# Low parts of the normalized tiles all on VectorE; norm sums, statistics and vector products rearranged through PSUM

## The chip, the cores and the metric

The kernel runs on one core of a Trainium2 chip. The metric is the device time of one execution in microseconds (us); lower is better. The program is one launch that works through two stacked networks of two layers each.

## The reference

```
# block 1, two layers (x: 512 tokens x 1024 features)
h = x @ w_in                         # split into three mixers' inputs
mix = concat(stick_breaking(h_sb), latent_attention(h_mla), rwkv7(h_rwkv)) @ w_o
x = layer_norm(ALPHA * x + mix, ln1_g, ln1_b)            # norms 0 and 2
u_act, u_gate = split(x @ ffn_w_up)
hid = gelu(causal_conv3(u_act)) * u_gate
x = layer_norm(ALPHA * x + hid @ ffn_w_down, ln2_g, ln2_b)  # norms 1 and 3
# block 2, two layers
h = modulate(rms_norm(x)); x = x + gate * mixer(h)       # norms 4 and 6; RG-LRU, then pooling
h = modulate(rms_norm(x)); x = x + gate * relu(h @ w1)**2 @ w2   # norms 5 and 7
out = rms_norm(x)                                        # norm 8
layer_norm(x) = (x - mean) * rsqrt(var + eps) * g + b    # over the 1024 features
```

## The kernel before, in words

**Layout.** Features lie on the partitions: `x` is 8 tiles of 128 features x 512 tokens. A weight matrix comes from HBM as a stream of chunks; a chunk holds 8 blocks of 128x128, by which it makes one tile of 128 output features. Two slots (`raw[:, 0]` and `raw[:, 1]`) alternate.

**Split products.** Each product is made of three fast ones (`split_product`, L668 to L670): both operands are split into a high part (`wh`, `xh`, `hidh`, rounded to fp32r) and a low part (`wl`, `xl`, `hidl`, the rest), and high x high, high x low and low x high are added up in PSUM. ScalarE makes `wh` of a chunk from `raw` (L1538, a whole chunk; L1552 and L1564, half chunks), then VectorE makes `wl` (L2361; L2374 and L2387, half chunks). `lo_done` tells TensorE and the DMA queue that a chunk is split.

**Order.** Each engine runs its own program, written out by hand, and engines meet at counting semaphores. Within a dense stretch TensorE works on two PSUM banks in turn, `dbank[0]` for even and `dbank[1]` for odd chunks (`dense`); before it writes a bank it waits on `bank_free[j]`, which whoever reads the bank last counts up.

**The deferred norms (0, 1, 2 and 5).** The first two chunks behind a norm are not made from the normalized input. `ahead_pair` multiplies `x * g` (not centred, not scaled) into `AHEAD` = `aux[0]`, `aux[1]` while the norm's sums are still being made; the missing terms follow from two vectors, `-g` and `b`, that are multiplied by the same weights. These vector products are two small matmuls behind each weight block (L793, L798: the weight block is loaded, 4 and 2 columns of `vcol` are streamed) and give columns in `COLS` = `aux[2]`. `ahead_out` adds the columns' parts (L2466) and computes `(x_product + mean * col) * rstd` into `ahead_t` (L2458, L2459). After the first half of a chunk TensorE counts `pe_half`, so ScalarE and VectorE can split the first half of the chunk after next (`early_half`); the rest follows after `pe_chunk` (`rest`).
`spread` (L772) is a matmul with a matrix of ones that adds 128 partitions' sums and spreads them: sum of `x` to `aux[5]`, sum of squares to `aux[4]`. `turned_pair` then multiplies the next two chunks into `TURNED` = `aux[3]`, `aux[4]`, in order of the tiles: for each normalized tile both chunks' blocks. After that TensorE makes chunks 5 and 6 of the stage (counted from 1) in `dbank[0]` and `dbank[1]`, each in one go, and before the change waits in front of them only for readers of before the norm (`pl.use(s + j, 1) - 2`).
`turned_tiles` on VectorE makes the tiles: `centre` (L2422, x - mean), `scale` (L2489, x g rstd), the low part `xl` (L2499); ScalarE makes `xh` with `b` (L1628).

**GpSimd's part.** It adds up `norm_sum` (L3333) and, for norm 1 and others, `norm_sq` (L3341). In norms 0 and 2 the squares' sum is VectorE's (L2967). GpSimd also makes three of the eight low parts, tiles 1, 3 and 5 (`POOL_LOW`; L3324), for which ScalarE first adds `b` to `x` itself (L1631). For the other five tiles ScalarE does that afterwards (`shift_tile`, L1641).

**Who reads the turned banks.** In the feed-forward of layers 1 and 2, VectorE reads `TURNED[1]` as the gate of hidden tile 1 (L3047). In layer 2's projections ScalarE reads it into `sbq` (L1729), behind the two `cq` (L1694), `ckv` (L1697), the five shifts (L1641), a wait for GpSimd's copy of the layer's vectors (L3352, which itself waits for the shifts) and three squares (L1711 to L1713). In norm 5's stage ScalarE reads it in a Relu (L2281).

Of the kernel before, what the change touches and what calls it, by code (L numbers as in the profile page):

```python
# [18 lines left out]
F32 = mybir.dt.float32  # L19
# [100 lines left out]
def columns(vecs):  # L120
    at, out = 0, {}
    for name, n in vecs:
# [10 lines left out]
          ("eye2", 64), ("tri", 64), ("tri_incl", 64), ("upper_half", 1),  # L133
# [4 lines left out]
def constants():  # L138
# [12 lines left out]
    put("ones", np.ones((P, P)))  # L151
    r, t = i % HD, np.arange(HD)[None, :]
# [29 lines left out]
POOL_LOW = (1, 3, 5)  # L182
# [5 lines left out]
SUMS = (8, 8, 8, 8, 7, 8, 7, 0, 7)  # L188
SQ_SUMS = (7, 8, 7, 8)
# [80 lines left out]
def build(nc, x_in, stream, mod_stream, vecs1, vecs2, consts, bands, c_rows, out):  # L270
    ctx = ExitStack()
    with ctx:
# [50 lines left out]
        ahead_t = at("ahead_t", [P, 2, S], krv_at + 18432)  # L323
        wag_at = top[0]
# [150 lines left out]
        tile_used, ahead_ready = sem("tile_used"), sem("ahead_ready")  # L475
        mean_ready, mean_pe, centred_x = sem("mean_ready"), sem("mean_pe"), sem("centred_x")
# [27 lines left out]
        lb_masked, n_masked, lk_masked = sem("lb_masked"), sem("n_masked"), sem("lk_masked")  # L504
        eye_ready, pb_zero, inv_turned = sem("eye_ready"), sem("pb_zero"), sem("inv_turned")
# [24 lines left out]
        z_pe, z_out, pool_pe, sq_pe = sem("z_pe"), sem("z_out"), sem("pool_pe"), sem("sq_pe")  # L530
# [32 lines left out]
        AHEAD, TURNED, COLS = (aux[0], aux[1]), (aux[3], aux[4]), aux[2]  # L563
# [98 lines left out]
        def _(pe):  # L662
# [101 lines left out]
            def spread(k, square):  # L764

                if k in (0, 2) and square:
                    pe.wait_ge(sq_added, sq_sums_before(k) + 7)
# [8 lines left out]
            def ahead_pair(pl, s, n, k):  # L776
# [3 lines left out]
                mine = slice(0, 4) if k < 4 else slice(1, 4, 2)  # L780
                ours = slice(0, 2) if k < 4 else mine
                n_hi = 4 if k < 4 else 2
                pe.wait_ge(vec_ready, vecs_split(k))
                for half in range(2):
                    for j in range(2):
                        if half == 0:
                            pe.wait_ge(lo_done, pl.chunk(s + j) + 1)
                        for t in range(4 * half, 4 * half + 4):
                            if j == 0:
                                pe.wait_ge(xl_ready, low0 + t + 1)  # L790
                            split_product(AHEAD[j][:], ((s + j) % 2, t * P), slice(0, P),
                                          (h[:, t, :], l[:, t, :]), t == 0, t == KT - 1)
                            m = pe.matmul(COLS[:, 8 * j:8 * j + n_hi], wh[:, (s + j) % 2, t, :],  # L793
                                          vcol[:, t, mine], start=t == 0 and j == 0, stop=False,
                                          skip_group_check=True)
                            if j == 1 and k in IN_PLACE:
                                m.then_inc(tile_used, 1)
                            m = pe.matmul(COLS[:, 8 * j:8 * j + 2], wl[:, (s + j) % 2, t, :],  # L798
                                          vcol[:, t, ours], start=False, stop=t == KT - 1,
                                          skip_group_check=True)  # L800
                        m.then_inc(pe_half if half == 0 else pe_chunk, 1)
                        if half == 0 and j == 0 and k < 4:
                            spread(k, False)
                    if half == 0:
                        spread(k, True)

            def turned_pair(pl, s, n, tile):

                q = halves(n)
                for t in range(KT):  # L810
                    tile(t)
                    for j in range(2):
                        if t == 0:
                            pe.wait_ge(lo_half, 2 * q + j + 1)
                        if t == 4:
                            pe.wait_ge(lo_done, pl.chunk(s + j) + 1)
# [15 lines left out]
            def deferred(pl, s, n, k, count, tile):  # L832

                ahead_pair(pl, s, n, k)
                turned_pair(pl, s + 2, n, tile)
# [325 lines left out]
            def inverses(L, pl):  # L1161
# [36 lines left out]
                pe.wait_ge(pb_zero, L + 1)  # L1198
# [34 lines left out]
            def scan_chunks(L, b):  # L1233
# [6 lines left out]
                pe.wait_ge(lb_masked, k + 1)  # L1240
# [36 lines left out]
                pe.wait_ge(lk_masked, k + 1)  # L1277
# [47 lines left out]
            for L in range(DEPTH):  # L1325
# [5 lines left out]
                elif 1 in DEFERRED:  # L1331
                    behind = 2
                    ahead_pair(pl, C_MLA, L * 2, 1)
                    turned_pair(pl, C_MLA + 2, L * 2, shared_low(lows_before(1, True), 3))
# [152 lines left out]
            def pool_sums(m):  # L1487
# [3 lines left out]
                    .then_inc(sums_pe if m == KT - 1 else sq_pe, 1)  # L1491
# [37 lines left out]
        def _(act):  # L1529
# [37 lines left out]
            def square(k, m):  # L1567
# [3 lines left out]
                elif k in (0, 2):  # L1571
                    act.wait_ge(sq_added, sq_sums_before(k) + max(1, m - 2))
# [15 lines left out]
            def mean_stats(k):  # L1588

                act.wait_ge(mean_pe, k + 1)  # L1590
                act.activation(mean_t[:], aux[5][:], ACT.Copy, scale=1.0 / D)\
                    .then_inc(mean_ready, 1)
                act.activation(var_t[:], aux[5][:], ACT.Square, scale=1.0 / D)\
                    .then_inc(mean_ready, 1)

            def root_stats(k):
# [4 lines left out]
                act.activation(rstd_t[:], var_t[:], ACT.Exp, scale=-0.5).then_inc(rstd_ready, 1)  # L1601
# [13 lines left out]
            def between(pl, s, q, m):  # L1615

                if m in (0, 2):
                    rest(pl, s + m // 2)
# [3 lines left out]
            def turned_tiles(k, b, pl, s, q):  # L1622

                for m in range(KT):
# [8 lines left out]
                    between(pl, s, q, m)  # L1633
# [47 lines left out]
            def projections(L, pl):  # L1681
                behind = 2 if L and 1 in DEFERRED else 0
                if behind:
                    q = halves(L * 2)
                    early_half(pl, C_MLA, q, 0)
                    mean_stats(1)
                    early_half(pl, C_MLA, q, 1)
# [4 lines left out]
                    for j in range(2):  # L1692
                        act.wait_ge(ahead_ready, 2 * deferred_before(1) + j + 1)
                        act.activation(cq[:, j, :], ahead_t[:, j, :], ACT.Identity,  # L1694
                                       bias=small[:, 12, 4 * j + 1:4 * j + 2])\
# [240 lines left out]
            def scan_chunks(L):  # L1936
# [7 lines left out]
                for b in range(BLOCKS):  # L1944
                    act.wait_ge(p_pe, L * 4 + b + 1)
                    act.wait_ge(pb_zero, L + 1)
# [67 lines left out]
            for L in range(DEPTH):  # L2014
# [19 lines left out]
                if ahead:  # L2034
                    up = C_FFN[0][0]
                    early_half(pl, up, q, 0)
                    mean_stats(k)
                    early_half(pl, up, q, 1)
# [7 lines left out]
                for g, tiles in enumerate(GROUPS1):  # L2046
                    up, down = C_FFN[g]
                    for i in range(tiles):
# [11 lines left out]
                        if early_chunks and i == 0:  # L2060
                            act.wait_ge(ahead_ready, 2 * deferred_before(k) + 1)
                            act.activation(cv[:], ahead_t[:, 0, :], ACT.Identity,
                                           scale=vec("conv2", 0), bias=small[:, 12, 2:3])
# [20 lines left out]
                        if g == 0 and ahead and i >= 3:  # L2084
# [1495 lines left out]
```

## Time and profile before

| | us |
|---|---|
| median of 3 runs | 2384.37 (2382.88 to 2385.79) |
| the profiled execution's own time | 2383.53 |
| its span, first to last instruction | 2381.7 |
| TensorE busy | 2309.4 (97%) |
| VectorE busy | 1450.3 (61%) |
| ScalarE busy | 1028.9 (43%) |
| GpSimd busy | 276.2 (12%) |
| mean granted TensorE clock | 0.989 of full |

"Busy" counts the time in which an engine has an instruction in work; matmuls overlap, so a busy TensorE can still run at half its clock. The time outside the span is 1.8 us.

### The profile page before, as it was taken

What the parts mean: (1) busy time and instruction counts of PE and PEld (TensorE: products, weight loads), DVE (VectorE), ACT (ScalarE), POOL (GpSimd) and SP (SyncE); (2) the same over time, 40 slices, a digit from 0 to 9 for tenths busy, and PEclk for the clock granted to TensorE, in tenths of its full rate; (3) what the DMA queues carried; (4) which work ended last, traced back from release to release, by engine and by line L of the source; (5) the groups of instructions that cost most, each with busy time, mean ns of one, the idle gap of its engine ahead of it and who ended that gap; (6) DMA issues with size and microseconds to landing.
All of it is one profiled execution on the core that took longest, in us unless ns stands there. A gap on an engine that the chain in (4) does not pass through costs nothing.

```text
span 2381.7 us, 35746 instructions
## 1 busy us (share of the span) xinstructions
PE 2309.4 (97%) x13360; PEld 1856.7 (78%) x13360; DVE 1450.3 (61%) x1970; ACT 1028.9 (43%) x1603; POOL 276.2 (12%) x199
## 2 busy tenths in 40 slices
PE   8999999999999999999999998999999999999998
PEld 6777767888887777767888876778888888888887
DVE  4668678666577678688666556577444356443443
ACT  5667245333345667245333334665233243332332
POOL 0042221000042141220000040201000010000001
PEclk9999999999999999999999997999999999999999
DMA  4210014555432210014555431222322221223222
GB/s 162 80 62 28 29 45 159 194 194 193 162 106 82 87 54 28 29 45 168 197 191 193 159 109 36 80 94 94 106 96 94 94 96 62 89 97 97 97 97 88
DMA packets 68797, 248.33 MB, mean 104 GB/s; under 512 B 7632, under 2 KB 8144, under 8 KB 68688
## 3 DMA queue, kind: packets, MB, share of 16 engines
q1 hardware_dynamic: 68688, 246.85, 31.1%
q8 instruction: 72, 1.18, 0.2%
q14 instruction: 37, 0.30, 0.0%
HBM read 244.72 MB, written 2.10 MB: 104 GB/s over the span
## 4 chain that ended last, share of the span: by engine, by line
PE 48%; DVE 4%; ACT 2%; issue 1%; DVEq 0%; ACTq 0%
PE dense L668 15%; PE dense L669 14%; PE dense L670 14%; PE aux L853 1%; PE aux L668 1%; ACT wh L1538 1%; PE aux L669 1%; PE aux L670 1%; DVE wl L2361 1%; DVE xc L3116 0%; DVE xc L3083 0%; DVE xc L3082 0%; DVE xc L3081 0%; PE aux L1483 0%; DVE hidl L2396 0%
## 5 line engine op out<-in xcount | busy, mean ns | idle before, releaser
L1538 ACT ACTIVATE wh<-raw 128x1024 fp32r<-128x1024 f32 x338 | 358.0, 1059 | 866.9 <-PE dense L670 858.4
L668 PE MATMUL dense<-xh,wh 128*128 128x512 f32 x1712 | 685.1, 400 | 16.4 <-DVE wl L2361 11.5
L2361 DVE TENSOR_TENSOR wl<-raw,wh 128x1024 fp32r<-128x1024 f32 x338 | 427.1, 1264 | 410.7 <-ACT wh L1538 408.8
L670 PE MATMUL dense<-xh,wl 128*128 128x512 f32 x1712 | 668.0, 390 | 0.0
L669 PE MATMUL dense<-xl,wh 128*128 128x512 f32 x1712 | 667.5, 390 | 0.0
L668 PEld LDWEIGHTS dense<-xh,wh 128*128 128x128 f32 x1712 | 322.1, 188 | 104.1 <-issue 25.9
L669 PEld LDWEIGHTS dense<-xl,wh 128*128 128x128 f32 x1712 | 322.4, 188 | 69.4 <-issue 5.8
L670 PEld LDWEIGHTS dense<-xh,wl 128*128 128x128 f32 x1712 | 321.8, 188 | 68.0
L668 PE MATMUL dense<-hidh,wh 128*128 128x512 f32 x928 | 362.9, 391 | 4.9 <-DVE hidl L2396 2.1
L669 PE MATMUL dense<-hidl,wh 128*128 128x512 f32 x928 | 361.2, 389 | 0.0
L670 PE MATMUL dense<-hidh,wl 128*128 128x512 f32 x928 | 361.2, 389 | 0.0
L668 PEld LDWEIGHTS dense<-hidh,wh 128*128 128x128 f32 x928 | 174.1, 188 | 46.5 <-DVE hidl L2396 7.3
L670 PEld LDWEIGHTS dense<-hidh,wl 128*128 128x128 f32 x928 | 174.2, 188 | 36.4
L669 PEld LDWEIGHTS dense<-hidl,wh 128*128 128x128 f32 x928 | 174.2, 188 | 35.8
L3227 DVE SCALAR_TENSOR_TENSOR x<-dense,mod,x 128x512 f32 (+1 forms) x64 | 48.0, 751 | 179.7 <-PE dense L670 179.7
L3341 POOL TENSOR_TENSOR norm_sq<-norm_sq,sq 128x512 f32<-128x512 f32 x38 | 69.1, 1818 | 721.5 <-ACT sq L1577 721.5
L3005 DVE CUSTOM_DVE_ANT_0 mraw<-mraw,cond 128x1024 f32<-128x1024 f32 x96 | 117.0, 1218 | 0.0
L3333 POOL TENSOR_TENSOR norm_sum<-norm_sum,x 128x512 f32<-128x512 f32 x32 | 55.1, 1723 | 520.6 <-DVE x L2923 492.0
L2012 ACT ACTIVATE hidh<-hf 128x512 f32 (+1 forms) x108 | 68.1, 631 | 99.1 <-DVE hf L3203 92.7
L2396 DVE TENSOR_TENSOR hidl<-hf,hidh 128x512 f32 (+1 forms) x108 | 74.4, 689 | 59.8 <-ACT hidh L2012 59.8
L1577 ACT ACTIVATE sq<-x 128x512 f32<-128x512 f32 x64 | 39.9, 624 | 48.3 <-DVE x L2977 20.3
L668 PE MATMUL aux<-xh,wh 128*128 128x512 f32 x96 | 42.5, 442 | 5.5 <-POOL xl L3324 5.5
(445 smaller groups left out, 2745.0 us busy)
## 6 DMA issues: line engine op xcount, KB each, us to landing
raw<-stream SPq DMA_DIRECT2D x362, 512.0 KB, 3.4
mraw<-mod_stream SPq DMA_DIRECT2D x96, 512.0 KB, 4.3
x<-x_t SPq DMA_DIRECT2D x4, 512.0 KB, 7.0
y_t<-x SPq DMA_DIRECT2D x8, 256.0 KB, 2.0
cst<-consts SPq DMA_DIRECT2D x1, 993.0 KB, 9.3
band<-bands SPq DMA_DIRECT2D x1, 576.0 KB, 4.4
cond<-c_rows SPq DMA_DIRECT2D x1, 512.0 KB, 10.6
pv_next<-vecs SPq DMA_DIRECT2D x3, 82.5 KB, 4.5
```

Of the source, the lines that this page charges most:

```text
L668: pe.matmul(o, a, h, start=first, stop=False)
L669: pe.matmul(o, a, l, start=False, stop=False)
L670: return pe.matmul(o, b, h, start=False, stop=last)
L1538: act.activation(wh[:, slot].rearrange("p k m -> p (k m)"), raw[:, slot, :], ACT.Copy).then_inc(hi_done, 1)
L1577: act.activation(sq[:, m % 2, :], x[:, m, :], ACT.Square).then_inc(sq_ready, 1)
L2012: act.activation(hidh[:, slot_i, :], hf[:, j, :], ACT.Copy).then_inc(hidh_ready, 1)
L2361: tt(wl[:, slot].rearrange("p k m -> p (k m)"), raw[:, slot, :], wh[:, slot].rearrange("p k m -> p (k m)").bitcast(F32), SUB)\
L2396: tt(dst, src, hi.bitcast(F32), SUB).then_inc(ready, 1)
L3005: dve.tensor_tensor_reduce(mraw[:, j, :], mraw[:, j, :], cond[:], 1.0, 0.0, MUL, ADD, mod_col[:, m:m + 1])\
L3227: stt(x[:, m, :], dbank[j][:], mod[:, lay, bass.ds(40 + m, 1)], x[:, m, :], MUL, ADD).then_inc(bank_free[j], 1)
L3333: pool.tensor_tensor(norm_sum[:], norm_sum[:], x[:, m, :], ALU.add)\
L3341: pool.tensor_tensor(norm_sq[:], norm_sq[:], sq[:, m % 2, :], ALU.add)\
```

## The change

- **PSUM operands.** The mean is read by `centre` from where `spread` left it (`MEAN` = `aux[5]`), and 1/std is written to `RSTD` = `aux[4]` and read there by `scale` and others. `aux[4]` is thus no longer free for the second turned chunk: `TURNED` becomes `aux[3]`, `dbank[1]`, and TensorE waits for its reader before the stage's chunk 6.
- **Mixers' sums.** In norms 0 and 2 VectorE makes both running sums, of `x` and of squares, in PSUM (`aux[3]`, `aux[4]`). In exchange GpSimd makes `wl` of four chunks there, the last two of `w_o` and the first two of the feed-forward.
- **Turned vector products.** Behind each half of `ahead_pair`, `vector_rows` loads the 4 (or 2) columns of `vcol` and streams both chunks' blocks, 256 columns; ScalarE copies the rows (`rows_out`), and two small matmuls in `turned_pair` turn them into columns. `pe_half` and `pe_chunk` are counted for both chunks together, behind these.
- **Low parts.** `POOL_LOW` is empty: VectorE makes all eight; ScalarE's shifts are eight.
- `turned_tiles` centres six tiles ahead rather than five, and the places of the half chunks' splits move. The sums' semaphore of norm 7 changes its name only.

```diff
-POOL_LOW = (1, 3, 5)
+POOL_LOW = ()
-        AHEAD, TURNED, COLS = (aux[0], aux[1]), (aux[3], aux[4]), aux[2]
+        AHEAD, TURNED, COLS = (aux[0], aux[1]), (aux[3], dbank[1]), aux[2]
+        MEAN, RSTD = aux[5], aux[4]
...
-                    pe.wait_ge(bank_free[j], pl.use(s + j, 1) - 2)
+                    pe.wait_ge(bank_free[j], pl.use(s + j, 1) - 2 + 2 * j)
...
+            def vector_rows(k, half):
+                mine = slice(0, 4) if k < 4 else slice(1, 4, 2)
+                n = 4 if k < 4 else 2
+                for t in range(4 * half, 4 * half + 4):
+                    pe.matmul(COLS[0:n, 0:2 * P], vcol[:, t, mine], wh[:, :, t, :],
+                              start=t == 0, stop=False)
+                    m = pe.matmul(COLS[0:2, 0:2 * P], vcol[:, t, mine][:, 0:2], wl[:, :, t, :],
+                                  start=False, stop=t == KT - 1)
+                return m
...
+            def vector_columns(k):
+                pe.wait_ge(rows_read, deferred_before(k) + 1)
...
+                for j in range(2):
+                    m = pe.matmul(COLS[:, 256 + 2 * j:258 + 2 * j], rows_t[0:n, P * j:P * j + P],
+                                  ones, start=j == 0, stop=True, skip_group_check=True)
...
-                tt(x[:, m, :], x[:, m, :], mean_t[:], SUB).then_inc(centred_x, 1)
+                stt(x[:, m, :], MEAN[:], -1.0 / D, x[:, m, :], MUL, ADD).then_inc(centred_x, 1)
...
-                early_half(q, 0)
-                for m in range(3):
+                lead = 6
+                for m in range(4):
                     centre(k, m)
                 variance_tile(k)
-                early_half(q, 1)
-                lead = 5
-                for m in range(3, lead):
+                for j in range(2):
+                    early_half(q, j)
+                for m in range(4, lead):
                     centre(k, m)
...
+                def tile_sum(m):
+                    if m > 1:
+                        dve.wait_ge(sq_added, sq_sums_before(k) + 2 * m - 3)
+                    dve.wait_ge(*x_added(k, m))
+                    tt(norm_sum[:] if m == KT - 1 else aux[3][:], x[:, m, :],
+                       x[:, 0, :] if m == 1 else aux[3][:], ADD).then_inc(sq_added, 1)
...
-                        if e and (ahead or a < 3):
-                            refill(pl, C_WO + 4 + a)
                         if m >= 2:
                             square_sum(m - 1)
-                        if ahead and m:
+                        if m:
+                            tile_sum(m)
                             ahead_lo(k, m - 1, vec("ln1_g", m - 1))
...
+            def low_weights(n, slot):
+                pool.wait_ge(hi_done, n + 1)
+                pool.wait_ge(lo_done, n)
+                pool.tensor_tensor(wl[:, slot].rearrange("p k m -> p (k m)"), raw[:, slot, :],
+                                   wh[:, slot].rearrange("p k m -> p (k m)").bitcast(F32),
+                                   ALU.subtract).then_inc(lo_done, 1)
...
-                sum_tiles(L * 2)
+                for a in range(4):
+                    n = place1(L).chunk(C_WO + 6 + a)
+                    low_weights(n, a % 2)
```

## Rows read from the trace of the kernel before

**Rows 1.** The page: busy time, share and instructions of each engine.
```profile
PE 2309.4 (97%) x13360; PEld 1856.7 (78%) x13360; DVE 1450.3 (61%) x1970; ACT 1028.9 (43%) x1603; POOL 276.2 (12%) x199
```
**Rows 2.** TensorE's waits, whole span: us in total, times, longest us.
```profile
PE aux L772 <- POOL norm_sum L3333: 7.5, 3, 2.7
PE aux L668 <- POOL xl L3324: 5.5, 9, 0.7
```
**Rows 3.** Norm 0 on TensorE's timeline: start us, us, engine, line [idle before].
```profile
345.33 2.08 PE L772 MATMUL aux<-norm_sum,cst 128*128 128x512 f32 x2 [2.70 <-POOL norm_sum L3333]
...
359.94 0.48 PE L668 MATMUL aux<-hidh,wh 128*128 128x512 f32 x1
...
360.86 0.48 PE L668 MATMUL aux<-xh,wh 128*128 128x512 f32 x1
...
374.60 0.39 PE L668 MATMUL dense<-xh,wh 128*128 128x512 f32 x1
...
375.28 0.39 PE L668 MATMUL dense<-xh,wh 128*128 128x512 f32 x1
...
386.10 0.49 PE L668 MATMUL dense<-xh,wh 128*128 128x512 f32 x1 [0.46 <-DVE wl L2361]
```
**Rows 4.** Windows: length, busy (instructions) of PE, PEld, DVE, ACT, POOL; PEclk, DMA.
```profile
345.30:349.00 3.70, 3.67 (x8) 2.35 (x9) 3.70 (x7) 1.08 (x2) 0.00 (x0) 0.50 0.48 143
...
1058.50:1060.00 1.50, 1.50 (x4) 0.85 (x3) 1.50 (x4) 0.56 (x2) 0.00 (x0) 0.50 0.55 224
```
**Rows 5.** Timeline, VectorE beside GpSimd, norms 0 and 1.
```profile
326.50 1.78 DVE L2445 SCALAR_TENSOR_TENSOR hidl<-x,pv,hidh 128x512 fp32r<-128x512 f32 x1
...
326.06 1.68 POOL L3333 TENSOR_TENSOR norm_sum<-norm_sum,x 128x512 f32<-128x512 f32 x1 [2.43 <-DVE x L2977]
...
694.07 1.74 POOL L3341 TENSOR_TENSOR norm_sq<-norm_sq,sq 128x512 f32<-128x512 f32 x1
694.58 0.68 DVE L2923 TENSOR_TENSOR x<-x,dense 128x512 f32<-128x512 f32 x1
...
699.72 1.29 POOL L3333 TENSOR_TENSOR norm_sum<-norm_sum,x 128x512 f32<-128x512 f32 x1
```
**Rows 6.** VectorE's timeline in norm 0.
```profile
342.34 0.67 DVE L2977 TENSOR_TENSOR x<-x,dense 128x512 f32<-128x512 f32 x1
...
356.75 0.74 DVE L2489 SCALAR_TENSOR_TENSOR x<-x,pv,rstd_t 128x512 f32<-128x512 f32 x1
357.42 0.68 DVE L2422 TENSOR_TENSOR x<-x,mean_t 128x512 f32<-128x512 f32 x1
358.02 0.75 DVE L2489 SCALAR_TENSOR_TENSOR x<-x,pv,rstd_t 128x512 f32<-128x512 f32 x1
```
**Rows 7.** TensorE's timeline later: matmuls of 256 columns in the pooling mixer.
```profile
1986.07 0.28 PE L1443 MATMUL aux<-wh,shift_h 128*128 128x256 f32 x1
1986.18 0.28 PE L1444 MATMUL aux<-wl,shift_h 128*128 128x256 f32 x1
```
**Rows 8.** The second turned bank's reader, norm 0; marks of norm 2.
```profile
383.88 0.69 DVE L3047 TENSOR_TENSOR hf<-gel,aux 128x512 f32<-128x512 f32 x1 [0.29 <-ACT gel L2082]
...
1054.56 0.67 DVE L2977 TENSOR_TENSOR x<-x,dense 128x512 f32<-128x512 f32 x1
...
1085.68 0.39 PE L668 MATMUL dense<-xh,wh 128*128 128x512 f32 x1
```
**Rows 9.** The same for norm 1: end of the turned pair, ScalarE's row of work.
```profile
745.03 0.39 PE L668 MATMUL dense<-xh,wh 128*128 128x512 f32 x1
...
749.50 3.17 ACT L1641 ACTIVATE x<-x,pv 128x512 f32<-128x512 f32 x5
...
755.35 0.57 ACT L1729 ACTIVATE sbq<-aux 128x512 f32<-128x512 f32 x1
```
**Rows 10.** The same for norm 5.
```profile
1655.31 0.39 PE L668 MATMUL dense<-xh,wh 128*128 128x512 f32 x1
...
1662.05 0.58 ACT L2281 ACTIVATE gel<-aux 128x512 f32<-128x512 f32 x1
```

More of the change, by code:

```diff
@@ L764, in spread @@
             def spread(k, square):
-                if k in (0, 2) and square:
-                    pe.wait_ge(sq_added, sq_sums_before(k) + 7)
+                if k in (0, 2):
+                    pe.wait_ge(sq_added, sq_sums_before(k) + (14 if square else 13))
                 elif k < 4 and square:
@@ L790, in ahead_pair @@
                                 pe.wait_ge(xl_ready, low0 + t + 1)
[L791 to L795, printed above, removed]
+                            m = split_product(AHEAD[j][:], ((s + j) % 2, t * P), slice(0, P),
+                                              (h[:, t, :], l[:, t, :]), t == 0, t == KT - 1)
@@ L1613, in ahead_hi, with between @@
                     .then_inc(xh_ready, 1)
-            def between(pl, s, q, m):
-                if m in (0, 2):
-                    rest(pl, s + m // 2)
+            def between(pl, s, q, m, k):
+                if m in (1, 2):
+                    rest(pl, s + m - 1)
+                    if m == 2:
+                        rows_out(k)
                 elif m >= 6:
@@ L2035, in _ @@
                     up = C_FFN[0][0]
-                    early_half(pl, up, q, 0)
                     mean_stats(k)
-                    early_half(pl, up, q, 1)
+                    for j in range(2):
+                        early_half(pl, up, q, j)
                     root_stats(k)
@@ L2062, in _ @@
                             act.activation(cv[:], ahead_t[:, 0, :], ACT.Identity,
-                                           scale=vec("conv2", 0), bias=small[:, 12, 2:3])
+                                           scale=vec("conv2", 0), bias=small[:, 12, 4:5])
                             act.wait_ge(conv_done, t)
@@ L2083, in _ @@
                            .then_inc(gel_ready, 1)
-                        if g == 0 and ahead and i >= 3:
-                            shift_tile(k, i - 3, "ln1_b")
+                        if g == 0 and ahead and i >= 4:
+                            for n in (2 * i - 8, 2 * i - 7):
+                                shift_tile(k, n, "ln1_b")
                     hidden_hi(bank_free[1], pl.use(up + 1, tiles - 1) + 1, tiles - 1, 0)
@@ L2122, in modulated @@
                     if behind is not None:
-                        between(*behind, m)
+                        between(*behind, m, k)
             act.wait_ge(fold_ready, 1)
@@ L3313, in clear_sums @@
                 if k in (0, 2):
-                    chain(pool.memset(norm_sum[:], 0.0))
                     return
```

144 lines of the change are left out of this document (74 added, 70 removed).

## The prediction

> **What bounds the kernel now.** I read the page first: TensorE is busy 97% of the span, the next engine 61% [rows 1]. So a microsecond counts only where TensorE waits, works more or less, or runs at half clock. TensorE's waits come next: GpSimd's sum of `x` holds it 7.5 us in three places, GpSimd's low parts 5.5 us in nine [rows 2]. Both are what this change goes for, and both lie at the norms. So I read norm 0's timeline, engine by engine, and looked for the same marks at norms 1, 2 and 5. The marks are the sum's matmul, the start and the end of the turned pair, and the last reader of the second turned bank. In norm 0 the first three are 345.33, 360.86 and 374.60 [rows 3]; the reader ends at 383.88 + 0.69 = 384.57 [rows 8]. After the 2.70 us wait the granted clock is 0.50, which is 1.2 of 2.4 GHz, for at least 3.7 us, and norm 2 shows the same [rows 4].
>
> **Vector products.** With the two vector matmuls a weight block takes 0.92 us, without them 0.68 [rows 3]: 0.24 for each of 16 blocks, 3.8 us a norm. After, 16 matmuls stream 256 columns. The nearest row, with 128 loaded columns, has them 0.11 apart [rows 7]: 1.8 us, so 2.0 less on TensorE per norm. No row shows a load of 4 columns; at no load cost it would be little less, at 0.24 each nothing is won. I take 0.11. What they gain counts only if the tiles are there when TensorE arrives; see below.
>
> **VectorE beside GpSimd.** The low part at 326.50 takes 1.78 us while GpSimd's sum (326.06 to 327.74) runs, against 0.74 or so alone; the add with a PSUM operand at 694.58 takes 0.68 though GpSimd is at work [rows 5]. So each GpSimd instruction shuts out VectorE's instructions with two SBUF operands and not those with one. VectorE's own steps are 0.60 for an add and 0.67 for a scale, from start to start [rows 6]. GpSimd alone needs 1.29 for 512 elements [rows 5]. It has no row for 1024; between once and twice that I take 2.5, because the work doubles.
> The Trainium skill, GPSIMD Engine Reference, section Engine selection, says that VectorE should do two-input elementwise work because GpSimd is about 2x slower; the trace agrees (1.29 against 0.60), and by this rule the four weight splits moved to GpSimd are a loss, which is the last rival below.
>
> **Norms 0 and 2 up to the turned pair's end.** Per column tile VectorE has after the change: x add 0.60, squares' sum 0.60, tile sum 0.60, low part 0.66, so 2.46; TensorE needs 12 steps of 0.2275 (a third of 0.68), 2.73. Before it was 2.43 (with half a weight split, 1.15 a chunk) and two shut-outs of about 1.05 a chunk. Now the low part alone can be shut out, by a 2.5 us split per chunk. I laid these out from 315.8, where the second half of `w_o` begins. GpSimd's splits are ready at about 326.0, 331.4, 337.7 and 343.9, where TensorE asks at 326.7, 332.2, 338.4 and 343.7. The last x add starts at 340.8 (before 342.34 [rows 6]), the last tile sum ends at 342.7. TensorE, which has its first half chunk done at 341.1, starts the sum's matmul at 342.8 instead of 345.33: a wait of 1.7 us instead of 2.7. Behind it come 0.9 (sum), 2.7 (half chunk), 0.9 (vector rows), 0.9 (squares), 5.5 and 0.9: the ahead pair ends at 354.9, before 360.86.
> VectorE finishes its low parts at 345.8, four centres at 348.4, the variance at 350.0, two half splits at 351.2, two centres at 352.5. It has begun `scale` at 356.75 before [rows 6]. From there to the end of the last low part are 18 steps of 0.66 (8 scales, 8 low parts, 2 centres) and 3 half splits of 0.60, 13.7 us, and TensorE takes 1.4 more for its blocks: the turned pair ends at 352.5 + 15.2 = 367.7. VectorE, not TensorE, sets this pace in either kernel; that is why the 2.0 us of the vector products aren't added. Against 374.60 this is 6.9 us less. Norm 2 went from its last x add to the same mark in 31.1 us (1054.56 to 1085.68 [rows 8]), norm 0 in 32.3, so it gains 1.2 less, 5.8 with rounding. If the low parts were hardly shut out I would get 9.0 and 7.9; if PSUM sums are slower than 0.60 or the clock falls here too, 3 and 2.
>
> **Norms 1 and 5 up to the same mark.** Norm 1's sums stay with GpSimd, so the start of its statistics is as before. Both half splits now stand ahead of the first scale, which comes 0.7 later; three low parts more (2.0) against three shut-outs less (2.9), one centre moved forward (0.6). The pair ends at 743.1, before 745.03 [rows 9]: 1.9 gained. Norm 5 has no centring; 1.2 gained, from the squares' matmul that starts 0.8 earlier.
>
> **The wait for the second bank: what the change adds.** `TURNED[1]` is now `dbank[1]`, and the stage's sixth chunk goes to that bank, so TensorE waits until the turned bank is read. It gets there one chunk after the turned pair, 8 x 0.68 = 5.46 us. The readers:
> - Norm 0: before, the gate's product ended 384.57 - 374.60 = 10.0 us after the pair [rows 3, 8]. The chain between is unchanged but for 0.35 less in the columns, and VectorE is freed a little later relative to TensorE: 10.2. Wait 4.8. Norm 2 the same, 4.8. Queued behind the waiting matmul is all of TensorE's queue. The wait of 0.46 for a split that came next [rows 3] is swallowed in both: 0.9 back.
> - Norm 1: the copy into `sbq` ended at 755.92, 10.9 after the pair [rows 9]. ScalarE has eight shifts instead of five ahead of it, 3 x 0.63 (3.17 for five [rows 9]) = 1.9, and GpSimd's copy of the vectors waits for them too. With the rest of its chain it ends at 756.15, 13.1 after 743.1. Wait 7.6.
> - Norm 5: the fourth Relu ended 7.3 us after the pair (1662.63 - 1655.31 [rows 10]). Wait 2.0 with rounding.
> Together 19.2 us that no row of before shows, because there the bank was another. Nothing later takes it up: TensorE was busy behind each.
>
> **The clock.** A wait of 2.7 us was followed by 0.50 for 3.7 us or more in norm 0, and for 1.5 us or more in norm 2 [rows 4]; half speed over 2.6 to 5.7 us loses 1.3 to 2.8. I take 2.0 for each of the three long waits, 6.0, and nothing for norm 5. If none falls it is 0, if all four, 11.
>
> **Elsewhere.** Norm 3's centres cost 0.06 more each with a scalar in them: 0.2. The smaller edits (ScalarE's square from SBUF, the second copy of 1/std in norm 5, `rows_out`, two small matmuls in the turned pair, norm 7's semaphore) lie beside the waits for the tiles; without that cover they are 0.3 to 0.6 each.
>
> **The sum.** -6.9 - 5.8 - 1.9 - 1.2 - 0.9 + 19.2 + 6.0 + 0.2 = +8.7 us. The profiled execution took 2383.53 (span 2381.7), 0.84 under the median, so I give 2392.5 for the median, rounded between the two.
>
> **The rivals.**
> 1. Slower by the bank's wait, as above: 62%, own range 2387 to 2398.
> 2. Even: the sums gain their upper bounds (9.0 and 7.9) and the clock barely falls (1.0). -9.0 - 7.9 - 1.9 - 1.2 - 0.9 + 19.2 + 0.2 + 1.0 = -0.5, 2384. For it speaks that VectorE loses fewer shut-outs than GpSimd's time suggests if the two interleave well; against it, that a 2.7 us wait lowered the clock twice. 20%.
> 3. Faster: the reader of the turned bank comes before TensorE needs it, since VectorE and ScalarE are freed sooner. Without the waits and their clock it is -16.5, 2368. It decides once the four waits and what clock they cost are together under about 12 us. The rows of norms 0 and 1, 10.0 and 10.9 us where 5.46 are hidden, speak against it. 8%.
> 4. GpSimd's weight splits come late, as the page on GpSimd would have it: they are ready only 0.7 us ahead of need. If each takes 3.5 instead of 2.5, the residual stage gets 2 to 3 us longer in norms 0 and 2 each, +5, 2397. 10%.
>
> **Range and chances.** From rival 2's lower side to rival 4's upper: 2383 to 2399. About 0.2%, 4.8 us, is what a measurement can tell. Slower by more: most of 1 and all of 4, 0.69. Within: 2 and the rim of 1, 0.22. Faster: 3 and a little of 2, 0.09.
>
> **What would show it.** TensorE's waits have a new first row: dense matmul, released by VectorE's `hf` twice (about 4.8), ScalarE's `sbq` (7.6) and `gel` (2.0). The rows of GpSimd's `norm_sum` and `xl` go, all but norm 3's. The marks move to about 342.8, 354.9 and 367.7. The windows behind the new waits have a clock near 0.50. The prediction is wrong if the bank's reader ends within 5.5 us of the turned pair, if VectorE's adds into PSUM take much over 0.68, or if GpSimd's split of 1024 elements is far from 2.5.

## The result and the profile after

The changed kernel takes 2389.6 us, the kernel before 2382.9 us (medians of 20 runs each in the same sitting). The ratio is 1.0030 with a 95% interval of 1.0024 to 1.0036: slower by 0.3%, or 7 us. The prediction was 2392.5 us and slower. The profiled execution has a span of 2386.8 us against 2381.7, 5.1 more.

The page of the changed kernel, its first part, beside [rows 1]:

```profile
PE 2307.3 (97%) x13312; PEld 1850.1 (78%) x13312; DVE 1438.1 (60%) x1975; ACT 1031.2 (43%) x1608; POOL 241.3 (10%) x180
```

TensorE is still the bound. TensorE's waits after (us in total, times, longest us), to be held against [rows 2]:

```profile
PE dense L673 <- DVE hf L3079: 8.7, 2, 4.4
PE dense L673 <- ACT sbq L1760: 6.9, 1, 6.9
...
PE aux L777 <- POOL norm_sum L3372: 3.1, 2, 2.1
...
PE dense L673 <- ACT gel L2313: 2.5, 2, 1.9
PE aux L777 <- DVE norm_sum L2996: 2.1, 2, 1.1
...
PE aux L673 <- DVE xl L2528: 0.8, 3, 0.3
...
PE aux L821 <- DVE xl L2528: 0.6, 3, 0.2
```

What the change goes for did shrink: the waits for GpSimd's low parts (5.5 us before) are 1.4 us on VectorE, those for the sum of `x` in norms 0 and 2 are 1.1 each, from 2.7. Norm 1 has a small wait for GpSimd's sum that the kernel before has not (3.1 us in two places, of which 2.12 are norm 3's as before), since TensorE comes to it earlier. But three rows are new: a dense matmul that waits for the reader of the second turned bank, 8.7 + 6.9 + 1.9 (the longer of the two for `gel`) = 17.5 us.

Norm 0 on TensorE's timeline (start, length, [idle before]), beside [rows 3]. It is the sum's matmul, the vector rows, the start and the last triple of the turned pair, and the chunk that goes to `dense1`:

```profile
342.04 1.12 PE L777 MATMUL aux<-norm_sum,cst 128*128 128x512 f32 x2 [1.06 <-DVE norm_sum L2996]
...
345.95 0.28 PE L809 MATMUL aux<-wh,vcol 128*4 128x256 f32 x1
346.07 0.28 PE L811 MATMUL aux<-wl,vcol 128*2 128x256 f32 x1
...
354.19 0.50 PE L673 MATMUL aux<-xh,wh 128*128 128x512 f32 x1
...
366.66 0.39 PE L675 MATMUL dense<-xh,wl 128*128 128x512 f32 x1
...
376.79 0.77 PE L673 MATMUL dense<-xh,wh 128*128 128x512 f32 x1 [4.29 <-DVE hf L3079]
```

The turned pair is over at 366.89 instead of 374.60, and then 4.29 us are given back at once. What comes in and behind the waits is in the windows (length, busy, PEclk, DMA share, GB/s):

```profile
372.50:376.70 4.20, 0.00 (x0) 0.75 0.71 256
376.79:381.50 4.71, 4.71 (x11) 0.50 0.32 111
381.50:384.50 3.00, 3.00 (x14) 1.00 0.52 175
747.20:750.00 2.80, 0.00 (x0) 1.00 0.00 0
750.20:754.00 3.80, 0.00 (x0) 0.50 0.00 0
754.10:756.50 2.40, 2.40 (x6) 0.50 0.00 0
...
1092.71:1097.50 4.79, 4.79 (x11) 0.50 0.32 109
1665.43:1670.50 5.07, 5.07 (x22) 1.00 0.08 14
```

Behind the waits of norms 0, 1 and 2 the granted clock is 0.50 (1.2 of 2.4 GHz), and 11 matmuls stand in 4.7 us where at full clock 21 would. Behind norm 5's wait of 1.86 us it is 1.00. The clock falls inside the wait: in norm 1 it reads 1.00 up to 750.0 and 0.50 from 750.2, while TensorE stands idle until 754.10; in norm 0 the 0.75 of the first window is 1.00 up to 374.6 and 0.50 behind.

The readers themselves, beside [rows 8 to 10]. Norm 0's gate product on VectorE; norm 1's eight shifts and the copy on ScalarE; norm 5's fourth Relu:

```profile
375.95 0.69 DVE L3079 TENSOR_TENSOR hf<-gel,dense 128x512 f32<-128x512 f32 x1 [0.29 <-ACT gel L2113]
```

```profile
745.72 4.99 ACT L1672 ACTIVATE x<-x,pv 128x512 f32<-128x512 f32 x8
751.81 0.63 ACT L1742 ACTIVATE csq<-cq 128x512 f32<-128x512 f32 x1 [1.09 <-POOL one_minus L3389]
...
753.38 0.57 ACT L1760 ACTIVATE sbq<-dense 128x512 f32<-128x512 f32 x1
```

```profile
1664.71 0.58 ACT L2313 ACTIVATE gel<-dense 128x512 f32<-128x512 f32 x1
```

GpSimd and VectorE side by side in norm 0, beside [rows 5, 6]:

```profile
322.32 2.48 POOL L3362 TENSOR_TENSOR wl<-raw,wh 128x1024 fp32r<-128x1024 f32 x1 [6.79 <-ACT wh L1560]
322.45 2.90 DVE L2477 SCALAR_TENSOR_TENSOR hidl<-x,pv,hidh 128x512 fp32r<-128x512 f32 x1
...
340.12 0.68 DVE L3014 TENSOR_TENSOR x<-x,dense 128x512 f32<-128x512 f32 x1
340.64 2.36 POOL L3362 TENSOR_TENSOR wl<-raw,wh 128x1024 fp32r<-128x1024 f32 x1 [3.46 <-ACT wh L1560]
340.71 0.68 DVE L3004 TENSOR_TENSOR aux<-sq,aux 128x512 f32<-128x512 f32 x1
...
341.31 0.68 DVE L2996 TENSOR_TENSOR norm_sum<-x,aux 128x512 f32<-128x512 f32 x1
```

A low part, all of whose tiles are in SBUF, ends only after GpSimd's split (2.90 us against 0.74 alone). The sums with a PSUM operand keep their 0.68 while GpSimd works at 340.64.

**A staircase.** The most useful view here is worked out, not read: for each kind of TensorE instruction both traces have, its start in one trace minus its start in the other, over the span. It is flat where both kernels take the same time, and has a step where one lost something. Each norm's step reaches from ahead of its first product to behind the chunks that follow its turned pair. "Elsewhere" is the rest of the span. In us:

```
pair of traces                      norm 0  norm 1  norm 2  norm 5  elsewhere  all
before -> after                       -1.3    +6.8    +0.4    +1.5     -2.4    +5.0
  of it, up to the turned pair's end  -7.3    -1.8    -6.1    -0.3
  of it, bank's wait and clock        +6.0    +8.5    +6.5    +1.8
after  -> e1_mean_bank                -6.3    -7.2    -6.8    -1.7     +1.1   -20.9
before -> e1_mean_bank                -7.6    -0.5    -6.4    -0.3     -1.1   -15.9
before -> e2_before_bank              +4.5    +8.5    +5.5    +1.8     +0.5   +20.8
after  -> e4_early_reader             -0.1    -6.8    +0.1    +0.1     -1.6    -8.3
after  -> e5_busy_wait                -2.3    -1.5    -2.6     0.0     +2.3    -4.1
e1     -> e6_low_on_gpsimd            +0.4    -0.8    +0.4    +0.1     +0.4    +0.5
e1     -> e8_weights_on_vector        +0.8    -0.1    +2.4    +0.1     +0.6    +3.8
e1     -> e9_sums_on_gpsimd           +5.3    +0.1    +4.3     0.0     -1.1    +8.6
e1     -> e11_sbuf_operands           +0.1    +0.1    +0.6     0.0      0.0    +0.8
e1     -> e12_vectors_as_before       +0.7    +0.5    +0.5    +0.3     +3.8    +5.8
e1     -> e10_waits_moved             -0.5    -1.9    -0.2     0.0     +0.7    -1.9
```

"Elsewhere" is mostly in three places that the experiments' edits do not touch. Near 100 us it is 1.5 us: from 93 to 99 us the granted clock is 0.72 in the traces of e1, e6, e8 and e11 and 1.00 in the other eight. Near 285 us, and near 1000 us in the scan of the second layer, TensorE has waits that the profile puts down to no other engine ("issue"); they differ by up to 2 us from kernel to kernel. There is one trace of each kernel, so they can't say whether such a place belongs to a kernel or to one execution. A difference of two profiled spans is thus uncertain by some 2 to 4 us as a measure of an edit (the column has -2.4 to +3.8), and a step at a norm by much less (norms 1 and 5 stay within 0.1 in e8 and e9, whose edits lie at norms 0 and 2).

### The profile page after: what moved, and what is told of

Its sections match the earlier page's. It is cut to its first block, busy times and chain, and to the rows that moved or that the text cites. A ratio compares the mean times of both kernels' runs of the same rounds, so it can differ in the third digit from the quotient of the medians.

```text
span 2386.8 us, 35656 instructions
## 1 busy us (share of the span) xinstructions
PE 2307.3 (97%) x13312; PEld 1850.1 (78%) x13312; DVE 1438.1 (60%) x1975; ACT 1031.2 (43%) x1608; POOL 241.3 (10%) x180
## 4 chain that ended last, share of the span: by engine, by line
PE 83%; DVE 8%; issue 4%; ACT 4%; DMA 0%; POOL 0%; DVEq 0%; ACTq 0%; SPq 0%; POOLq 0%
PE dense L673 23%; PE dense L675 23%; PE dense L674 23%; ACT wh L1560 1%; PE aux L875 1%; PE aux L673 1%; PE aux L674 1%; PE aux L675 1%; DVE wl L2393 1%; PE aux L1033 1%; DVE hidl L2477 1%; PE aux L1051 1%; PE aux L1154 1%; PE aux L1165 1%; PE aux L1021 1%
## 5 line engine op out<-in xcount | busy, mean ns | idle before, releaser
L673 PE MATMUL dense<-xh,wh 128*128 128x512 f32 x1744 | 699.9, 401 | 31.8 <-DVE wl L2393 10.5
L675 PE MATMUL dense<-xh,wl 128*128 128x512 f32 x1744 | 682.7, 391 | 0.0
L674 PE MATMUL dense<-xl,wh 128*128 128x512 f32 x1744 | 682.1, 391 | 0.0
L2393 DVE TENSOR_TENSOR wl<-raw,wh 128x1024 fp32r<-128x1024 f32 x330 | 415.0, 1258 | 430.3 <-ACT wh L1560 428.7
L673 PEld LDWEIGHTS dense<-xh,wh 128*128 128x128 f32 x1744 | 329.7, 189 | 120.8 <-issue 45.1
L674 PEld LDWEIGHTS dense<-xl,wh 128*128 128x128 f32 x1744 | 329.8, 189 | 71.2 <-issue 5.8
L675 PEld LDWEIGHTS dense<-xh,wl 128*128 128x128 f32 x1744 | 329.1, 189 | 69.9
L3372 POOL TENSOR_TENSOR norm_sum<-norm_sum,x 128x512 f32<-128x512 f32 x16 | 26.5, 1654 | 490.9 <-DVE x L2952 490.9
L2694 DVE TENSOR_TENSOR_SCAN later<-keep 128x127 f32<-128x127 f32 (+3 forms) x32 | 34.2, 1069 | 16.7 <-ACT sig L1826 13.1
```

Of the source, the lines that this page charges most:

```text
L673: pe.matmul(o, a, h, start=first, stop=False)
L674: pe.matmul(o, a, l, start=False, stop=False)
L675: return pe.matmul(o, b, h, start=False, stop=last)
L2393: tt(wl[:, slot].rearrange("p k m -> p (k m)"), raw[:, slot, :], wh[:, slot].rearrange("p k m -> p (k m)").bitcast(F32), SUB)\
L2694: chain(dve.tensor_tensor_scan(later[:, b, 0:n - 1][:, ::-1], k, k, 1.0, MUL, ALU.min))
```

## The experiments

All were timed in five rounds against the kernel before. Its medians beside them were 2383.4, 2383.8 and 2383.7 us.

### The bank

**e1_mean_bank**: the changed kernel with the second turned product in the bank of the mean. The first wait is that of the turned pair's first tile, the second that of the chunks behind it.

```
-AHEAD, TURNED, COLS = (aux[0], aux[1]), (aux[3], dbank[1]), aux[2]
+AHEAD, TURNED, COLS = (aux[0], aux[1]), (aux[3], aux[5]), aux[2]
...
-    if j == 1: pe.wait_ge(bank_free[1], pl.use(s + 1) - 1)
+    if j == 1 and k < 4: pe.wait_ge(centred_x, 8 * k + 8)
...
-    pe.wait_ge(bank_free[j], pl.use(s + j, 1) - 2 + 2 * j)
+    pe.wait_ge(bank_free[j], pl.use(s + j, 1) - 2)
```

> The changed kernel, but the second turned product goes to the bank that held the sums for the mean (read for the last time by the last centring) in place of dense 1, so that the next chunk needs no reader to be done. The theory (the waits for the second bank are the loss): all four go, 8.7 + 6.9 + 1.9 = 17.5 us, and the slow stretches of TensorE's clock behind three of them, about 6 us; against it stand up to 1 us in each of norms 0, 1 and 2 for the last centring, and about 1 us in norm 1, where the latent sums now ask for ScalarE's squares before they are there: 2366 to 2371 us. The rival (the readers' waits only took the place of others that are behind them, weight splits or landings): no change within 5 us, 2385 to 2390 us, with waits of like length under other names. The sum of the prediction also says that the edits of the norms alone are worth 16 us against the kernel before, so this one should be faster than before by 12 to 17 us.

2368.8 us; 0.9946 of the kernel before (0.9932 to 0.9959). All four waits are gone and nothing like them is behind. TensorE's waits of this kernel hold one new row, the squares of the latents in norm 1:

```profile
PE aux L926 <- ACT csq L1744: 1.2, 1, 1.2
```

So the bank costs 20.8 us (2389.6 - 2368.8), and without it the change is a gain of 14.6 us by the medians, 12.9 by the ratio, 15.9 in the traces. The rival of other waits behind these falls.

**e2_before_bank**: the same bank and its two waits put into the kernel before, nothing else.

```
-AHEAD, TURNED, COLS = (aux[0], aux[1]), (aux[3], aux[4]), aux[2]
+AHEAD, TURNED, COLS = (aux[0], aux[1]), (aux[3], dbank[1]), aux[2]
+    if j == 1: pe.wait_ge(bank_free[1], pl.use(s + 1) - 1)
...
-    pe.wait_ge(bank_free[j], pl.use(s + j, 1) - 2)
+    pe.wait_ge(bank_free[j], pl.use(s + j, 1) - 2 + 2 * j)
```

> The kernel before with one edit of the change alone: the second turned product goes to dense 1, with the two waits that this needs. The theory: the waits come as in the changed kernel, 4.5 us (norm 0), 5.4 (norm 1, with five shifts ahead of the reader and not eight), 4.7 (norm 2) and 1.9 (norm 5), 16.5 us in all, and 5 to 6 us of slow clock behind three of them: 2383 + 22 = 2405 us. The rival (the bank costs little in itself, the loss of the changed kernel is elsewhere, in GpSimd's weight splits or the longer VectorE): 2383 to 2388 us.

2404.2 us; 1.0092 (1.0076 to 1.0107). Norms 0 and 1 of this kernel on TensorE's timeline:

```profile
386.24 0.47 PE L668 MATMUL dense<-xh,wh 128*128 128x512 f32 x1 [4.50 <-DVE hf L3049]
...
763.26 0.77 PE L668 MATMUL dense<-xh,wh 128*128 128x512 f32 x1 [5.42 <-ACT sbq L1731]
```

Taking the bank away and putting it in give the same price, 20.8 us. That they agree to 0.1 is luck: the interval of e2 alone is 18 to 26 us, and at the four norms the traces have 22.0 taken away (e1) and 20.3 put in, with 17.5 and 16.3 us of waits. In norm 1 the wait is 5.42 us and not 6.94, with three shifts of 0.62 us fewer ahead of the copy.

**e4_early_reader**: the changed kernel with norm 1's copy ahead of the shifts.

```
     act.activation(ckv[:], TURNED[0][:], ACT.Copy).then_inc(bank_free[0], 1)
+    act.activation(sbq[:, 0, :], TURNED[1][:], ACT.Copy).then_inc(bank_free[1], 1)
     for n in range(len(OWN_LOW)):
         shift_tile(1, n, "ln2_b")
```

> The changed kernel, with ScalarE's copy out of the second turned bank in norm 1 moved ahead of its eight shifts. The theory: the wait of 6.9 us and the slow clock behind it (1.6 us) go, and a wait of about 1.4 us for the squares of the latents comes, since their three instructions still stand behind the shifts: 7 us less, 2382.5 us. The rival (the shifts are on the path anyway, by way of the squares and the weight split behind them): 2 us less or nothing, 2388 to 2390 us.

2383.6 us, 6.0 less than the changed kernel; 1.0001 of the one before (0.9992 to 1.001). The step is at norm 1 alone, -6.8: the wait of 6.9 us and its slow clock go, and one of 1.6 us for the squares of the latents comes, as expected. One line's place makes the change even.

**e5_busy_wait**: the waits stay, TensorE is kept at work in them.

```
+    if j == 1:
+        for _ in range({0: 4, 1: 7, 2: 4, 5: 1}[k]):
+            pe.matmul(aux[5][:], const("ident"), cst[:, 0:S], start=True, stop=True)
     pe.wait_ge(bank_free[j], pl.use(s + j, 1) - 2 + 2 * j)
```

> The changed kernel, with 4, 7, 4 and 1 matmuls of a constant into the bank of the mean put into TensorE's waits for the second bank in norms 0, 1, 2 and 5 (their output is read by nobody). The waits stay, but TensorE is not idle in them. The theory (the slow clock comes from the idle time and costs by itself): the granted clock stays at 1.0 behind them, and the time falls by 2.4 + 1.6 + 2.2 = 6 us to about 2383.5 us. The rival (the clock would fall there anyway, or the matmuls are longer than the waits): 2389 us or more.

2384.6 us, 5.0 less; 1.0007 (0.9998 to 1.0016). Norm 0 on its timeline, and the window from the same start:

```profile
373.60 3.60 PE L849 MATMUL aux<-cst 128*128 128x512 f32 x8
377.97 0.53 PE L673 MATMUL dense<-xh,wh 128*128 128x512 f32 x1 [0.78 <-DVE hf L3082]
```

```profile
377.97:382.97 5.00, 5.00 (x22) 1.00 0.32 105
```

The reader is as late as before (TensorE starts behind it 9.8 us after the end of the turned pair, against 9.9), but the clock is 1.00 and not 0.50. The steps are -2.3, -1.5 and -2.6, and none in norm 5: the clock's share of the loss is 6.4 us by the traces, 5.0 by the medians.

### The parts of the gain, undone one by one in the kernel without the bank's wait

**e6_low_on_gpsimd**: the edit that gives the change its name, undone.

```
-POOL_LOW = ()
+POOL_LOW = (1, 3, 5)
-if g == 0 and ahead and i >= 4:
-    for n in (2 * i - 8, 2 * i - 7):
-        shift_tile(k, n, "ln1_b")
+if g == 0 and ahead and i >= 3:
+    shift_tile(k, i - 3, "ln1_b")
```

> The kernel of e1_mean_bank (2368.8 us), with the low parts of tiles 1, 3 and 5 given back to GpSimd, and the shifts of the other five tiles spread as in the kernel before. The theory (a low part on GpSimd comes late to TensorE and shuts VectorE out as it goes): three waits of about 0.6 us in each of norms 0, 1 and 2, as in the kernel before, so 4 to 6 us more: 2373 to 2375 us. The rival (VectorE sets the pace of the turned pair, and three tiles less relieve it): 2366 to 2368 us.

2368.3 us against 2368.8; 0.9934 (0.9921 to 0.9948). My theory (2373 to 2375) missed; the rival's time fits, but not its reason. TensorE in norm 0, and GpSimd's part that it waits for:

```profile
358.83 0.50 PE L673 MATMUL aux<-xh,wh 128*128 128x512 f32 x1 [0.42 <-POOL xl L3354]
362.55 0.60 PE L821 MATMUL aux<-cst,rows_t 4*128 4x2 f32 x4 [0.70 <-POOL xl L3354]
```

```profile
360.80 1.69 POOL L3354 TENSOR_TENSOR xl<-x,xh 128x512 fp32r<-128x512 f32 x1 [2.02 <-ACT x L1662]
```

The waits are 1.1 us a norm, where VectorE's own low parts leave 0.5, so +0.4 in norms 0 and 2. In norm 1 it turns round (-0.8): with five shifts on ScalarE in place of eight the squares of the latents are there in time, and their 1.2 us go. The two cancel. That VectorE makes all eight low parts is worth nothing here.

**e8_weights_on_vector** and **e9_sums_on_gpsimd**: first the four late weight splits back on VectorE (below, VectorE's and GpSimd's parts), then the tile sums back on GpSimd as well: GpSimd calls `sum_tiles(L * 2)`, VectorE's `tile_sum(m)` goes, and the squares are summed in SBUF.

```
 tt(x[:, m, :], x[:, m, :], dbank[e][:], ADD).then_inc(bank_free[e], 1)
+if e:
+    refill(pl, C_WO + 4 + a)
...
-for a in range(4):
-    n = place1(L).chunk(C_WO + 6 + a)
-    low_weights(n, a % 2)
```

> The kernel of e1_mean_bank, with the low weights of the four late w_o chunks given back from GpSimd to VectorE, where the kernel before has them. VectorE then has four operations of 1.28 us more in each of norms 0 and 2, and its low parts of x are no longer stretched (by 5.6 us in norm 0). The theory (the two sums are about equal, but the last weight split stands between the last residual and the last tile sum): 1 to 3 us more in all, 2370 to 2372 us. The rival (what counts is that VectorE is shut out): 2 us less or better, under 2367 us.

> The kernel of e8_weights_on_vector, with the tile sums of norms 0 and 2 given back to GpSimd and the sums of squares back to SBUF. The theory (the sum's chain on GpSimd ends late): TensorE's wait for the sum grows from 1.0 to 2.7 us twice, with a slow clock behind it, and VectorE is shut out: 5 to 9 us more than e1_mean_bank, 2374 to 2378 us, most of the gain over the kernel before in these two norms. The rival (the sums are hidden, the gain came from the low parts and the turned vectors): within 2 us of e1_mean_bank.

2372.4 us (0.9955, 0.9941 to 0.9968) and 2376.1 us (0.9967, 0.9955 to 0.9979). The sum's matmul in e8, norms 0 and 2, the window behind the second, and the same matmul of norm 0 in e9 with GpSimd's last sum:

```profile
344.51 1.12 PE L777 MATMUL aux<-norm_sum,cst 128*128 128x512 f32 x2 [2.34 <-DVE norm_sum L2996]
...
1048.29 1.12 PE L777 MATMUL aux<-norm_sum,cst 128*128 128x512 f32 x2 [2.38 <-DVE norm_sum L2996]
```

```profile
1048.29:1051.00 2.71, 2.71 (x7) 0.71 0.53 181
```

```profile
346.19 2.08 PE L777 MATMUL aux<-norm_sum,cst 128*128 128x512 f32 x2 [3.52 <-POOL norm_sum L3374]
```

```profile
343.95 2.18 POOL L3374 TENSOR_TENSOR norm_sum<-norm_sum,x 128x512 f32<-128x512 f32 x1 [1.23 <-DVE x L3014]
```

The wait for the sum is 1.0 us with only tile sums on VectorE, 2.34 with a weight split of 1.21 us ahead of the last one, and 3.52 with the sum on GpSimd, whose last add takes 2.18. The steps at norms 0 and 2 are +3.2 for the splits and 9.6 - 3.2 = 6.4 more for the sums, slow clock included (0.50 over the 3.8 us behind the wait of 3.52). Both theories hold: e8 is 0.4 us above its range, and e9's wait grew to 3.5 us, not 2.7. Of the 3.2 us, 2.4 are norm 2's, where the clock fell behind the wait, and 0.8 norm 0's, where it did not. This pair of edits is most of the gain.

The Trainium skill, GPSIMD Engine Reference, section Engine selection, gives two-input elementwise work to VectorE, since GpSimd is about half as fast. The durations agree, 2.36 to 2.48 us against 1.21 for the split of 1024 elements; yet giving it to GpSimd won 3.2 us by the traces, because VectorE was what the sum waited for.

**e11_sbuf_operands**: mean and 1/std read from SBUF.

```
-MEAN, RSTD = aux[5], aux[4]
+MEAN, RSTD = aux[5], rstd_t
-stt(x[:, m, :], MEAN[:], -1.0 / D, x[:, m, :], MUL, ADD)
+tt(x[:, m, :], x[:, m, :], mean_t[:], SUB)
```

> The kernel of e1_mean_bank, with the mean and the reciprocal root read by VectorE from SBUF and not from PSUM. The theory (the operand's place changes nothing for VectorE in these stretches, since GpSimd does nothing there): within 2 us of e1_mean_bank, 2367 to 2371 us. The rival (the PSUM operands keep VectorE from being shut out and so carry part of the gain): 3 us more or worse.

2370.3 us; 0.9945 (0.9932 to 0.9959), within 0.0001 of e1's ratio, and 0.8 us in the traces. The theory holds: the operand's place is worth next to nothing where GpSimd is idle.

**e12_vectors_as_before**: 32 narrow products a norm in place of 16 rows of 256 columns.

```
-m = vector_rows(k, half)
+pe.matmul(COLS[:, 8 * j:8 * j + n_hi], wh[:, (s + j) % 2, t, :], vcol[:, t, mine], ...)
+pe.matmul(COLS[:, 8 * j:8 * j + 2], wl[:, (s + j) % 2, t, :], vcol[:, t, ours], ...)
```

> The kernel of e1_mean_bank (2368.8 us), with the vector products of the ahead pairs as in the kernel before: two narrow products with each of the 16 triples (32 in a norm), in place of 16 rows of 256 columns, the copy and four products with ones. The theory (this is the part of the gain that the norms without new sums show, where 1.9 us came in norm 1 and no more than 0.6 of it from the low parts): 1.2 to 1.5 us more in each of four norms, 2373 to 2375 us. The rival (the narrow products are hidden behind the weight loads of the triples and cost as little as the rows): 2368 to 2370 us; what then brought the gain in norm 1 is open.

2373.2 us; 0.995 (0.9937 to 0.9964). The medians are 4.4 us apart, the ratios only 0.9, and the staircase has 0.7, 0.5, 0.5 and 0.3 at the norms; its other 3.8 us are in places that the edit doesn't touch, 2.2 of them in the scan near 1000 us, where the kernel before has a like wait (see "What I left out" below). So the part is 2.0 us at the norms, and up to 4.4 if the scan's wait comes with the edit, which no run shows. Neither theory nor rival holds as written: the products are dearer than the rows, but most of what they cost is covered by the wait for VectorE's tiles.

**e10_waits_moved**: e1 with the waits left at the norms attacked: the edits of VectorE below, and in norm 1 ScalarE's order `cq`, `ckv`, `csq`, `sbq`, then the shifts, with the waits for `vecs_ready` behind the weight splits.

```
+if m == KT - 1:
+    tile_sum(m)
 if m >= 2:
     square_sum(m - 1)
...
-for m in range(4):
+for m in range(5):
     centre(k, m)
 variance_tile(k)
```

> The kernel of e1_mean_bank, with four waits that its trace shows attacked: the last tile sum of norms 0 and 2 goes ahead of the last but one sum of squares on VectorE (0.6 us of 1.04, twice), a fifth centring goes into VectorE's idle 0.8 us ahead of the variance (0.27 us before the turned pair, three times), and in norm 1 ScalarE squares the latents and copies the turned product ahead of the shifts, with the waits for the new layer's vectors moved behind the weight splits (1.15 us). The theory: all three come through, 3 us less than e1_mean_bank, 2366 us. The rival (each uncovers the next wait at the same place, the weight split of VectorE above all): within 1 us of e1_mean_bank.

2366.9 us; 0.9927 (0.9914 to 0.9941). The sum's wait in norm 0:

```profile
343.83 1.12 PE L777 MATMUL aux<-norm_sum,cst 128*128 128x512 f32 x2 [0.66 <-DVE norm_sum L2999]
```

It fell by 0.4 and not by 0.6, and 0.29 us for GpSimd's split appeared behind it, so that norms 0 and 2 gained 0.5 and 0.2 where the theory had 0.9 each: there the rival is right. In norm 1 the squares' wait went: -1.9. In sum 2.6 us at the norms, 1.9 by the medians. This is the fastest of all, 16.8 us faster than the kernel before.

## Why the prediction was right, step by step

- **The sign and its cause.** I forecast +8.7 us from 19.2 us of waits for the second bank and 6.0 of clock against 16.7 gained. Measured are +6.7 in the medians and +5.0 in the traces, with 17.5 us of waits. e1 and e2 settle the cause from both sides, some 21 us each. The time forecast, 2392.5, is 2.9 above the measured one; half of that is the kernel before, 2384.4 in its three runs and 2382.9 in this sitting.
- **Each wait.** Norm 0: 4.29 against 4.8; norm 2: 4.39 against 4.8; norm 1: 6.94 against 7.6; norm 5: 1.86 against 2.0, which is 7.3 us behind the pair (1665.29 - 1657.98) as forecast. The reader's distance from the turned pair was 376.64 - 366.89 = 9.75 us where I had 10.2, and 753.95 - 741.57 = 12.4 where I had 13.1. The chain behind the pair was somewhat shorter than I let it be in norms 0, 1 and 2; in norm 5 only the rounding was off. The two waits for a split that I took to be swallowed (0.9) are gone: 0.46 and 0.44 in norms 0 and 2 before, none after, and 0.19 each in e1.
- **The clock.** I took 2.0 us for each of three waits and nothing for norm 5. e5 shows 2.3, 1.5, 2.6 and 0 in the traces, 5.0 in the medians.
- **Norms 0 and 2 up to the turned pair's end.** -7.3 and -6.1 against -6.9 and -5.8. The marks of norm 0 were 342.04, 354.19 and 366.89; I had 342.8, 354.9 and 367.7, all 0.7 to 0.8 late. VectorE's scales start 1.0 earlier than laid out (351.48 against 352.5), its adds take 0.60 as assumed, and the sum's wait is 1.06 where I had 1.7. The clock is 1.00 behind it (342.6 to 345.2), where 0.50 stood behind the 2.70 us of before [rows 4]. GpSimd's split is 2.36 to 2.48 us (I took 2.5); it is not late, so rival 4 fell.
- **What in it gains.** By e9, e6 and e12 sums and weight splits give 9.6 us in the two norms, low parts 0.8, turned vectors 1.2 and the PSUM operands (e11) 0.7. That the vectors add little since VectorE sets the pace is borne out: 2.0 us over four norms, where TensorE alone would save 2.0 in each. The parts come to 12.3 of the 14.0 us by which e1 beats the kernel before in norms 0 and 2; the rest, the order of centres and half splits among it, I did not try alone. Nor do the parts simply add up: in e9 TensorE waits 3.52 us for GpSimd's sum where the kernel before waits 2.70, since without the vector products it comes there earlier.
- **Norm 1.** -1.8 against -1.9, but this agreement is luck in part: the terms that I wrote down (0.7 and 2.0 later, 2.9 and 0.6 earlier) come to 0.8, not 1.9. In the traces VectorE's first scale comes 0.6 later in the norm, as forecast, the way from there to its last low part is 1.8 shorter (12.89 against 14.65 us), and the pair ends 0.7 closer behind that low part (2.5 against 3.2).
- **Norm 5.** -0.3 against -1.2: this term was mis-sized. The trace shows where it went, though no run tried it alone. Measured from VectorE's low part ahead of it (1631.94 before, 1634.90 after), the turned pair starts 1.1 us earlier, but takes 11.87 us (1646.10 to 1657.97) where it took 11.03 (1644.28 to 1655.31). TensorE has no wait for tiles in it in either kernel, so the small matmuls that turn the columns have no cover here:

```profile
1644.28 0.48 PE L668 MATMUL aux<-xh,wh 128*128 128x512 f32 x1
```

```profile
1650.31 0.60 PE L821 MATMUL aux<-cst,rows_t 2*128 2x2 f32 x4
1650.85 0.50 PE L673 MATMUL aux<-xh,wh 128*128 128x512 f32 x1
```

I had named that price (0.3 to 0.6) but laid it beside waits for tiles. The squares' matmul, too, starts 0.2 earlier and not 0.8 (2.75 us later by the clock of the traces, where all is 2.96 later).
- **Norm 3.** +0.2 forecast, -0.6 in this pair of traces. Laid against the kernel before, nearly all traces are 0.4 to 0.6 shorter there, and that of e2 is too, whose norm 3 has none of the edits. So the 0.2 doesn't show, and what shows isn't explained.
- **What I left out.** -1.9 us in the scan of the second layer, where the trace before has two waits that the one after hasn't. This is the longer:

```profile
1003.11 0.59 PE L1322 MATMUL aux<-ysq,cst 128*128 128x512 f32 x1 [1.01 <-issue]
```

A wait of 1.0 to 1.5 us at this matmul is in the traces of the kernel before, of e2 and of e12, the three kernels with the old vector products, and in none of the other nine. So it doesn't look like chance, and it may be a small gain of the change; what causes it is open.
- **The rivals.** Rival 2 (even) wanted larger gains from the sums and little clock: the clock was there. Rival 3 (hidden readers) would have been 2368, and is about what e1 gives once the bank is another: 2368.8. Its sum, -16.5, counts as gained the 0.9 that only the long waits swallow; e1 has 0.4 of it again, and the traces give it -15.9.

## What to carry to other kernels

A product's bank is held until its last reader is done, so before moving a result to a bank of a rotating pair, measure how long after the product that reader ends: here 7.3 to 12.4 us, with 5.5 us of cover, and it undid a gain of 14.6 us. Look for a bank whose last reader is early (here the mean's), or move the reader ahead of work that nobody waits for; one copy ahead of eight shifts gave 6 us. When parts of a change are weighed, compare starts of the same instructions over the span: it separates a step of 0.5 us at the place of the edit from 2 us elsewhere, which the medians of five runs do not. And when a term of a sum is hidden behind a wait at one place, look whether the wait is there at each of the others; at norm 5 it was not.

## What the runs showed of the hardware

- A longer wait did not cost more in slow clock behind it: the clock is 0.50 for 4.7 us behind 4.29 us of idle TensorE, but only for 2.8 us behind 6.94. It fell inside both waits, about 2 and 4 us before their ends, so that in norm 1 more of the slow stretch passed while TensorE stood idle anyway. Behind 2.34 us of wait (e8, norm 0) the clock stayed 1.00; behind 2.38 us (norm 2 of the same kernel) it was 0.71 over 2.7 us. Matmuls that nobody reads, put into the wait, kept it at 1.00.
- Matmuls of 256 columns with a load of 4 or 2 columns start 0.11 to 0.12 us apart, no closer than those with 128 loaded columns [rows 7].
- GpSimd is slowed beside VectorE too: its adds of 512 elements take 1.68 and 2.18 to 2.32 us in e9 while VectorE works on tiles in SBUF, against 1.29 at its shortest [rows 5].
